# Two output tiles of a pair issued matmul by matmul in turn, in a two-layer block and a second block on one Trainium2 core

## What is computed

```python
def first_block(x, c, ...):
    for l in range(DEPTH):                       # DEPTH = 2
        h = rms_norm(x, g_pre_mix[l]) * (1 + sc_mix) + sh_mix
        y = mixer(h, w_in[l], ...)               # w_in, short and long convolution, mLSTM heads, w_out
        x = x + gt_mix * rms_norm(y, g_post_mix[l])
        h = rms_norm(x, g_pre_mlp[l]) * (1 + sc_mlp) + sh_mlp
        f = jnp.square(jax.nn.relu(h @ w_ff1[l])) @ w_ff2[l]
        x = x + gt_mlp * rms_norm(f, g_post_mlp[l])
```

## Time and profile before

| | us |
|---|---|
| median of 3 runs | 2851.8 |
| lowest and highest | 2850.62, 2855.81 |
| the profiled execution | 2854.71 |
| its span, first to last instruction | 2852.9 |

### The profile page before, as it was taken

One profiled execution on the slowest core, in us unless ns is written; L12 is line 12 of the kernel. 1 busy time (PEld: TensorE's weight loads), 2 busy tenths in 40 slices (PEclk: granted clock), 3 DMA queues, 4 the chain that ended last, 5 costly groups with the idle time before them and its releaser, 6 DMA issues.

```text
span 2852.9 us, 30642 instructions
## 1 busy us (share of the span) xinstructions
PE 2548.6 (89%) x10350; PEld 1925.3 (67%) x10350; DVE 1293.4 (45%) x2077; ACT 992.2 (35%) x1513; POOL 1110.0 (39%) x570
## 2 busy tenths in 40 slices
PE   2999788959999869977995999996998999899998
PEld 2787445748888658853574788884776767688886
DVE  4578844452322366895353422235547424312212
ACT  1325444332332232454342432233533322323322
POOL 2345262444444434625335344443432003444443
PEclk6999978979999979987897999997998559999999
DMA  6652100223333336310022233331321002233232
GB/s 209 200 162 83 45 1 15 81 67 96 121 121 125 114 127 206 96 46 15 1 67 81 82 125 119 123 94 44 88 82 52 1 1 72 69 96 95 90 95 74
DMA packets 219415, 248.36 MB, mean 87 GB/s; under 512 B 9818, under 2 KB 188826, under 8 KB 219290
## 3 DMA queue, kind: packets, MB, share of 16 engines
q1 hardware_dynamic: 219290, 246.84, 27.3%
HBM read 244.71 MB, written 2.10 MB: 87 GB/s over the span
## 4 chain that ended last, share of the span: by engine, by line
PE 77%; issue 9%; DVE 8%; ACT 3%; POOL 2%; PEld 2%; DMA 0%; POOLq 0%; DVEq 0%; PEldq 0%; ACTq 0%; SPq 0%
PE product L1811 21%; PE product L1813 20%; PE product L1812 20%; PE side L2141 3%; PE product L2163 2%; PE side L1852 2%; PE side L1975 2%; PE side L1858 1%; POOL slot_f L743 1%; PE product L2005 1%; PE side L2151 1%; DVE side L1357 1%; PE side L1871 1%; PE product L2015 1%; ACT va L860 1%
## 5 line engine op out<-in xcount | busy, mean ns | idle before, releaser
L734 POOL TENSOR_TENSOR ring_low<-ring_f,ring_high 128x1024 fp32r<-128x1024 f32 (+1 forms) x350 | 841.6, 2411 | 1382.7 <-ACT ring_high L819 1379.3
L1811 PE MATMUL product<-slot_r,ring_high 128*128 128x512 f32 x2792 | 1125.8, 403 | 58.9 <-DVE slot_r L1430 19.4
L1812 PE MATMUL product<-slot_r,ring_low 128*128 128x512 f32 x2792 | 1114.8, 399 | 0.0
L1813 PE MATMUL product<-slot_r,ring_high 128*128 128x512 f32 x2792 | 1114.0, 399 | 0.0
L1811 PEld LDWEIGHTS product<-slot_r,ring_high 128*128 128x128 f32 x2792 | 531.5, 190 | 218.4 <-issue 49.7
L819 ACT ACTIVATE ring_high<-ring_f 128x1024 fp32r<-128x1024 f32 (+1 forms) x350 | 367.7, 1053 | 758.7 <-DMA ring_f<-in_w_ff 320.7
L1813 PEld LDWEIGHTS product<-slot_r,ring_high 128*128 128x128 f32 x2792 | 531.2, 190 | 129.2
L1812 PEld LDWEIGHTS product<-slot_r,ring_low 128*128 128x128 f32 x2792 | 532.4, 191 | 124.2 <-issue 0.5
L1325 DVE SCALAR_TENSOR_TENSOR va<-product,sqt 128x512 f32<-128x512 f32 x96 | 66.1, 690 | 387.1 <-ACT sqt L873 387.1
L1357 DVE SCALAR_TENSOR_TENSOR side<-slot_f,cols,side 128x512 f32<-128x512 f32 x336 | 222.8, 744 | 0.0
L1335 DVE TENSOR_TENSOR slot_f<-product,slot_f 128x512 f32<-128x512 f32 x64 | 43.5, 691 | 228.5 <-PE product L1813 228.3
(11 more groups left out here) (244 smaller groups left out, 2173.0 us busy)
## 6 DMA issues: line engine op xcount, KB each, us to landing
ring_f<-in_w_ff SPq DMA_DIRECT2D x128, 512.0 KB, 3.6
slot_f<-in_w_ada SPq DMA_DIRECT2D x56, 1024.0 KB, 5.3
ring_f<-in_w_in SPq DMA_DIRECT2D x96, 512.0 KB, 3.8
ring_f<-in_w_out SPq DMA_DIRECT2D x40, 512.0 KB, 3.4
ring_f<-in_w_up SPq DMA_DIRECT2D x32, 512.0 KB, 3.6
ring_f<-in_w_down SPq DMA_DIRECT2D x32, 512.0 KB, 3.4
slot_f<-in_x SPq DMA_DIRECT2D x1, 2048.0 KB
ring_f<-in_w_v SPq DMA_DIRECT2D x4, 512.0 KB, 3.8
```

Source lines behind the costliest of these rows:

```text
L734: pool.tensor_tensor(ring_low[:, s, :, 0:n], ring_f[:, s, :, 0:n], ring_high[:, s, :, 0:n].bitcast(F32), ALU.subtract).then_inc(low_ready. ...
L1811: pe.matmul(out_ap, high, rhs_high, start=start, stop=False)
L1812: pe.matmul(out_ap, low, rhs_high, start=False, stop=False)
L1813: return pe.matmul(out_ap, high, rhs_low, start=False, stop=stop)
```

## The change

`use_pair` no longer calls `use_chunk`. It has a loop of its own in which the tile index is innermost: for each row block and each of the three parts, a matmul of tile `o` and then one of tile `o + 1`. Neighbouring matmuls so have the same activations, different weights and different PSUM banks. Both banks are waited for at the start of the pair, and the last matmul of each tile in each chunk still counts in `done`, in the same order.

```diff
             def use_pair(place, plan, i, o, slots, need=None):
 
                 for kh in range(2):
-                    use_chunk(place, plan, i + kh,
-                              [(o + m, [(kk, m * P, slots, KC * kh + kk) for kk in range(KC)], kh == 0, kh == 1)
-                               for m in range(2)], need)
+                    wait(pe, place, low_ready, plan.split(i + kh))
+                    s = chunk_slot(i + kh)
+                    if kh == 0:
+                        wait_bank(pe, place, o)
+                        wait_bank(pe, place, o + 1)
+                    for kk in range(KC):
+                        k = KC * kh + kk
+                        if need is not None:
+                            need(k)
+                        high, low = tile_r(slots[0], k), tile_r(slots[1], k)
+                        for n, (weights, rhs) in enumerate(((ring_high, high), (ring_low, high), (ring_high, low))):
+                            for m in range(2):
+                                ins = pe.matmul(bank(o + m)[:], weights[:, s, kk, m * P:(m + 1) * P], rhs,
+                                                start=k == 0 and n == 0, stop=k == NT - 1 and n == 2)
+                                if kk == KC - 1 and n == 2:
+                                    ins.then_inc(done.sem, 1)
```

## The result

The changed kernel takes 2894.81 us (median of 4 runs, 2890.64 to 2905.55), the kernel before 2853.81 beside it (2850.62 to 2857.92): ratio 1.0149, 95% interval 1.0116 to 1.0181. The forecast was 2858.3, its range ended at 2866. The sign was right and the size was not: +41 us by the medians, where +6.5 was forecast. The profiled execution is the slowest of the four, 2905.55 us with a span of 2903.7, so its rows hold some 10 us more than the median: the two traces differ by 50.8 us.

What follows compares the result with a forecast made beforehand. It took PE's stream of fast float32 matmuls, with gaps, as the bound. Terms +4.7 + 6.2 + 2.2 - 4.2 - 2.4 = +6.5 us on the 2851.8 median gave 2858.3 us; range 2855 to 2866.

Steps and rivals of the forecast that it cites:

- The stream, 0: PE's matmuls: as many matmuls, weight loads and waits as before, so no change; bounds 52 us gain, 8 us loss.
- the 139 us: PE's stream: by the skill's 215.7 ns per matmul, a stream freed of its excess would be 139 us shorter.
- The rival in which the bank costs: PE's matmuls: a steady run in one bank costs time, so up to 52 us gained, about 2806; chance 0.06.
- the one of cycling banks: PE's clock: cycling banks or longer waits cost clock; 2861 after one longer wait, 3010 if a tenth ran slow; chance 0.02.
- "Covered", 0, at most 2.4 us: Eight MLP groups: modulation 1.75 us later, at 679.33, PE wants it at 679.47; if uncovered, 0.3 us x 8.
- Its third sign, a granted clock under 0.90: Whole kernel: a granted clock under 0.90 was listed among the signs that the forecast is wrong.
- Convolutions, +4.7: Both layers' convolutions: ACT's copy 1.8 us later, then Silus behind the fifth sigmoid; +2.35 us for each layer.
- The wait for L1430: Convolutions: PE's wait for L1430 growing longer was listed among the signs that the forecast is right.
- Norms' ends, six at +6.2: Six norm ends: POOL's last sum later, +1.26 us at four, +1.0 at kernel's end, +0.15 at end of layer 0.
- Starts of `w_out`, -4.2: Where activations come tile by tile, PE asks more slowly and stalls less; pair 0 ends 2.1 us earlier, twice.
- Behind the rotary swaps, +2.2: A weight copy behind the rotary swaps: the second swap queues behind the first, +2.2 us, all on PE.
- MLP starts, -2.4: MLP starts: stalls with refills vanish, 0.95 us for the layers and some 0.25 in the second block's two starts.

Runs made afterwards that it cites:

- the run outside the MLP: Changed kernel's turns in every pair but those of the MLP, which keep the order of the kernel before: 2870.86 us, ratio 1.0053.
- the run with the PSUM operand: Changed kernel, with DVE's L1325 writing the activation to an idle PSUM bank instead of SBUF, read there by L890 and L1317: 2870.29 us, ratio 1.0047.
- first pairs: Kernel before, with turns only in the first pair of an up group, of `w_out` and of the second block's projections: 2852.85 us, ratio 0.9985.
- The kernel before with the PSUM operand: Kernel before, with the activation written to an idle PSUM bank instead of SBUF, order of matmuls unchanged: 2855.21 us, ratio 1.0008.
- the first chunk in turns: Against the kernel before, turns only in each pair's first chunk (24 of 48 matmuls), the second tile by tile: 2857.82 us, ratio 1.0008.

## Why the prediction was wrong

*The stream, 0:* right. The interval is 233.3 ns in both kernels, in the MLP and in the second block's MLP. (The 215.7 ns that the prediction sets beside it are, in the Trainium skill, TensorE: Matmul & The Clock Gate, Back-to-back issue gap, the gap of an isolated matmul; for a stream the page has other figures, so the 139 us do not follow from it.) The rival in which the bank costs is refuted over the whole kernel, and so is the one of cycling banks: no gap stands between alternating matmuls.

*"Covered", 0, at most 2.4 us:* this is the step that failed. It put the modulation 1.75 us later, 0.14 us inside PE's demand. The 1.75 was right as far as ACT's queue goes (1.8 measured at the last ReLU), but the step took DVE's durations from the trace of before as constants. The last two subtractions take 4.75 us in place of 1.67, another 3.1 us; the modulation came some 3 us late and not just in time. The gaps and the slow matmuls behind them were worth 30.8 us in the two MLPs of the profiled execution, in place of 0. The text had named the sign to look for ("waits for the modulation (L1237) in each MLP group, then the cover was misjudged"), and had priced it at 0.3 us a group; it was 3.9 in the mean. Its third sign, a granted clock under 0.90, could tell nothing: the kernel before has 0.897. The changed one has 0.887 to 0.892.

*A term that was not there:* the norms behind the MLPs. Their chains on DVE went from 3.79 to 8.12 and from 2.16 to 6.16 us, for the same reason. PE's shift grew by 3.4 and 3.9 us over them.

*Convolutions, +4.7:* +3.1 and +1.9 by the shifts, 5.0 together: the first place is right, the sum is in part luck. At the first place, where PE waits for L1425, the step is 2.3 and 2.4 us, as forecast (PE's waits went from 9.5 to 14.3 us). The wait for L1430, which the forecast had named as the sign, did not grow (19.4 and 19.3). The run outside the MLP has the same order here and loses only 0.5 and 0.1 us, for at L1430 it gets some 2 us back. In layer 0 the two are

```profile
298.65 7.27 POOL L734 TENSOR_TENSOR ring_low<-ring_f,ring_high 128x1024 fp32r<-128x1024 f32 x1 [3.45 <-ACT ring_high L819]
298.75 4.89 DVE L1430 TENSOR_TENSOR slot_r<-slot_f,slot_r 128x512 fp32r<-128x512 f32 x8
```

There the eight subtractions of L1430 run without a pause and POOL's low part takes 7.27 us; in the kernel before the low part takes 2.34 and the first L1430 waits for it, 2.06 us. Which of the two gets ahead the records do not tell here (POOL's begins 0.10 us before L1430's), and the forecast had no term for it.

*Norms' ends, six at +6.2:* right. From PE's last product to its first sum the shift grows by 1.24, 1.24, 1.23 and 1.23 us at the four places where 1.26 was forecast, by 1.18 at the kernel's end for 1.0, and by 0.03 at the end of layer 0 for 0.15: 6.15 us together.

*Starts of `w_out`, -4.2:* -2.1 in each layer, right. But the stage as a whole came out at -2.3 and -2.1, norms' ends included, where -0.8 each follows from the terms. A further gain of 3.1 us lies in both layers between the first pairs and the heads' norm, and a loss of 1.2 to 1.3 at that norm; neither was in the sum. The gain is the clock's: in the kernel before it is 0.51 and 0.50 over 499.8 to 504.9 and 1448.5 to 1453.6 us, some 12 products at 427 ns each, and in the changed kernel 1.00 at the same matmuls. The run with the PSUM operand has the same order and in layer 0 only half of the gain, so how much of it the steadier start brings is open. The loss is the lock again: of the two L1268 at that norm the first now takes 0.69 us and the second 2.58, beside a low part, where it was 1.32 and 0.68 (1.28 and 0.68 in layer 1).

*Behind the rotary swaps, +2.2:* PE's wait for the low part there went from 0.27 us to 2.4. The stage lost 2.2 us in the run outside the MLP, as forecast, and 3.7 in the changed kernel; the difference is no wait but slower matmuls behind it, which the forecast had left to a rival.

*MLP starts, -2.4:* with turns in the first pairs alone PE's shift falls by 0.7 us at the start of the first MLP and by 0.2 at the second's; the forecast had 0.95 for each. In the changed kernel this drowns in the loss.

Without the layers' MLPs and the norms behind them the forecast's terms come to 6.5 + 1.9 - 1.4 = 7.0, the profiled execution to 9.8, or 8.1 without the 1.7 of its start. That they lie so close is in part luck: the convolutions' race and the clock, gains and losses of 1 to 3 us each, nearly cancel. So the forecast was a fair account of ACT's queue and a wrong one of DVE, and its range held no case in which an instruction of unchanged shape takes up to four times as long. The row that could have told was on the page: L1317, 947 ns in the mean, stands beside L1325 at 690 ns for the same 512 columns. A mean that is 37% above its neighbour's is a reason to look for a mixture, and the trace by instruction would have shown 0.68 and 1.24.

## What to carry to other kernels

Before moving work in time, look at each instruction that would be moved for two durations of one shape; if there are two, the longer may be a neighbour's lock, and a shift of half a microsecond, or less, can add or remove it. Where DVE and GpSimd work at the same time, move operands of DVE to idle PSUM, above all in the small serial operations of a norm: 4 or 512 columns, each blocked one waited here for a GpSimd instruction of 2.4 us. One SBUF input in place of two is enough for `tensor_tensor` (0.68 us in 96 of 96); for `tensor_scalar` see below. And let the first tile of a pair end early: in this kernel the engines behind PE needed the space between two ends, and PE gained nothing from changing banks.

## What the hardware showed that I had not expected

A DVE operation on four columns (0.16 us) takes 2.25 to 2.34 us beside POOL's low parts, though it moves next to nothing. L1261 has only one SBUF input and is blocked too (2.33 us); with input and output in PSUM it takes 0.17. The Trainium skill (SBUF — State Buffer, Who interferes with whom) counts `tensor_scalar` among the operations that can take the shared pair; the trace agrees. The lock works both ways: a low part that starts while DVE's operation runs takes up to 2.93 us in place of 2.4 (25 of the 354 low parts in the changed kernel take 2.5 or more, 21 in the kernel before), and 7.27 beside eight DVE subtractions in a row.

A blocked DVE instruction goes on for 0.54 to 0.56 us after the low part ends, where the whole takes 0.68 alone. My reading is that it has been started and then waits; it would explain why the record is long and no idle time shows before it.

The clock has steps that the change does not explain. The kernel before with the PSUM operand loses 3.0 us between 2182 and 2365 us, where its code is unchanged: the clock over 2350 to 2365 is 0.50 there,

```profile
2350.00:2365.00 15.00, 13.76 (x57) 11.34 (x56) 3.39 (x7) 2.95 (x7) 0.00 (x0) 0.50 0.00 0
```

and 0.72 in the kernel before:

```profile
2350.00:2365.00 15.00, 12.44 (x65) 10.18 (x64) 4.11 (x10) 4.73 (x9) 0.33 (x1) 0.72 0.00 0
```

The changed kernel, the run outside the MLP and the one with the PSUM operand lose the same 3.0 us there; the first chunk in turns and first pairs do not. What sets which of the two a run gets is open; sums of single microseconds over this kernel carry that much doubt.
